# Modulation products moved out of the rounds of five attentions into the two merges of branches

## The reference, cut to what matters

```
# first block: four branches of width 1024
y_fox, y_lru, y_sb, y_mem = ...            # fox and stick-breaking attention, an LRU, memory attention
gates = sigmoid(h @ w_in[:, gates] + b_gate)             # [tokens, 4, 1024]
mixed = sum_n gates[n] * (branches[n] @ w_branch[n])
x = x + mixed @ w_out;  x = x + ffn(x)
# second block: two layers, i = 0, 1
mod  = silu(c)     @ w_ada[i] + b_ada[i]                 # 1024 -> 6 * 1024: shift, scale, gate, twice
modc = silu(c_ctx) @ w_ada[i] + b_ada[i]
h = modulate(rmsnorm(x), sh1, sc1); ...                  # na, da attention and gMLP, width 512 each
x = x + gt1 * ((ga * (ya @ wb[0]) + gb * (yb @ wb[1]) + gc * (yc @ wb[2])) @ w_out)
x = x + gt2 * ec_moe(modulate(rmsnorm(x), sh2, sc2))     # 16 experts
```

## Time and profile before

| | us |
|---|---|
| median of three runs | 3234.0 (3230.39 to 3244.86) |
| the profiled execution's own time | 3241.7 |
| its span in the profile | 3239.9 |
| first merge of branches | 192.0 |
| second merge (layer 0) | 199.0 |
| fox, na_x and da_x attention (layer 0) | 66.9, 64.4, 55.3 |
| mean granted clock of TensorE | 0.925 |

### The profile page before, as it was taken

How to read it: one execution, slowest core, us unless ns; L and a number is a source line. 1 busy time by engine, 2 the same in 40 slices (tenths; PEclk the granted TensorE clock), 3 DMA queues, 4 the chain that set the end, 5 groups by cost and what they waited for, 6 DMA issues and landing times. The chain is left out here.

```text
span 3239.9 us, 36546 instructions
## 1 busy us (share of the span) xinstructions
PE 2658.2 (82%) x14364; PEld 1796.3 (55%) x14364; DVE 1169.5 (36%) x1596; ACT 882.3 (27%) x1314; POOL 39.9 (1%) x36
## 2 busy tenths in 40 slices
PE   6887898998998787889977778887887896787876
PEld 5666687998996464668753222223664894222222
DVE  4446544655753334344432001103444552000001
ACT  3344433544442232322221000002233432000001
POOL 0100000000000000000000000000000001000000
PEclk8888998999998898889978999998897997999999
DMA  4463532453542333112215999996211343999996
GB/s 154 157 257 113 198 130 92 178 185 123 188 159 91 150 136 130 50 69 100 85 46 224 404 405 407 403 414 260 78 52 50 142 165 147 413 410 409 411 410 269
DMA packets 92935, 669.19 MB, mean 207 GB/s; under 512 B 10320, under 2 KB 10496, under 8 KB 12800
## 3 DMA queue, kind: packets, MB, share of 16 engines
q1 hardware_dynamic: 90256, 654.67, 51.6%
q0 software_dynamic: 2272, 11.52, 1.0%
q10 hardware_dynamic: 272, 1.05, 0.1%
HBM read 666.13 MB, written 1.06 MB: 206 GB/s over the span
## 5 line engine op out<-in xcount | busy, mean ns | idle before, releaser
L1860 PE MATMUL ps<-ring,WK 128*64 128x512 f32 x3072 | 731.0, 605 | 171.2 <-DMA ring<-in_stream 147.1
L424 PE MATMUL ps<-A,piece_hi 128*128 128x256 f32 (+1 forms) x1952 | 618.5, 317 | 97.7 <-DVEq L358 33.1
L376 DVE TENSOR_TENSOR ring_lo<-ring,piece_hi 128x1024 fp32r<-128x1024 f32 x378 | 459.3, 1220 | 450.4 <-ACT piece_hi L369 449.3
L425 PE MATMUL ps<-A,piece_hi 128*128 128x256 f32 (+1 forms) x1952 | 612.5, 314 | 0.0
L426 PE MATMUL ps<-A,ring_lo 128*128 128x256 f32 (+1 forms) x1952 | 611.7, 313 | 0.0
L1860 PEld LDWEIGHTS ps<-ring,WK 128*64 128x64 f32 x3072 | 194.5, 137 | 674.2 <-DMA ring<-in_stream 371.9
L424 PEld LDWEIGHTS ps<-A,piece_hi 128*128 128x128 f32 x1952 | 384.7, 197 | 129.3 <-issue 59.2
L369 ACT ACTIVATE piece_hi<-ring 128x1024 fp32r<-128x1024 f32 x378 | 388.2, 1053 | 223.8 <-DVEq L450 131.9
L425 PEld LDWEIGHTS ps<-A,piece_hi 128*128 128x128 f32 x1952 | 385.6, 198 | 17.2
L426 PEld LDWEIGHTS ps<-A,ring_lo 128*128 128x128 f32 x1952 | 384.9, 197 | 18.1
L1980 DVE TENSOR_TENSOR WK<-WK,ps 128x512 f32<-128x512 f32 x32 | 22.0, 688 | 636.7 <-PE ps L1860 636.7
(11 more groups left out here) (252 smaller groups left out, 2447.6 us busy)
## 6 DMA issues: line engine op xcount, KB each, us to landing
ring<-in_stream SPq DMA_DIRECT2D x621, 1024.0 KB, 7.7
WK<-in_na_bias POOLq DMA_DIRECT2D x2, 2048.0 KB, 7.8
WK<-cum_scratch POOLq DMA_DIRECT2D x1, 2048.0 KB, 9.7
const<-in_const SPq DMA_DIRECT2D x1, 1267.0 KB, 11.7
WK<-in_x SPq DMA_DIRECT2D x1, 1024.0 KB, 5.4
WK<-in_mem SPq DMA_DIRECT2D x1, 1024.0 KB, 9.1
WK<-cum_scratch POOLq DMA_DIRECT2D x1, 1024.0 KB, 14.9
WK<-in_lru_w POOLq DMA_DIRECT2D x1, 1024.0 KB, 5.1
```

Of the source, the lines that this page charges most:

```text
L376: nc.vector.tensor_tensor(ring_lo[:, slot, at:at + PIECE], ring[:, slot, at:at + PIECE], f32(piece_hi[:, j, :]), ALU.subtract).then_inc(lo ...
L424: nc.tensor.matmul(out_, l[0], r[0], start=first, stop=False)
L425: nc.tensor.matmul(out_, l[0], r[1], start=False, stop=False)
L1860: last = nc.tensor.matmul(ps[64 * n:64 * n + 64, bank, :], lhs, piece[:, n * 512:n * 512 + 512], start=(k == 0), stop=(k == DC - 1))
```

## The change

The 48 steps of the modulation leave the attentions. A step now follows two split pieces in a merge: 32 steps (four groups, three of layer 0 and the first of layer 1) behind every pair of pieces of the first merge, 16 (two groups) behind the first 16 of 18 pairs of the second. The stream is laid out to match, so that in the first merge every slot of split pieces is followed by a slot of raw ones. `next_piece` and `split_ahead` pass over the raw pieces: still AHEAD = 3 split pieces in front. In these merges the banks go round among six, and the modulation uses banks 6 and 7 in turn. `ada_dve` stands behind each second piece in VectorE's list. The turn and the bias of a group follow one pair later. The first merge is no longer a hardware loop. R, AHEAD and SyncE's code stay as they are.

```diff
+ADA_GROUPS = {0: ((0, 0), (0, 1), (0, 2), (1, 0)), 1: ((1, 1), (1, 2))}
+ADA_NO = {group: n for n, group in enumerate(ADA_GROUPS[0] + ADA_GROUPS[1])}
+def ada_step(merge, slot):
+
+    return (*ADA_GROUPS[merge][slot // DC], slot % DC) if slot < DC * len(ADA_GROUPS[merge]) else None
...
+    def merge(m, slots):
+        nonlocal at
+        for slot in range(slots):
+            at += 2
+            if ada_step(m, slot):
+                RAW[at:at + 2] = ADA
+                at += 2
+                if ada_step(m, slot)[2] == DC - 1:
+                    ADA_LAST[ada_step(m, slot)[:2]] = at - 1
+    merge(0, 32)
+    at += BLOCK_PIECES - 22 * 4 - 64 + 32
+    merge(1, 18)
...
+SPLIT_AT = [p for p in range(PIECES) if RAW[p] == SPLIT]
+SPLIT_NO = np.concatenate([[0], np.cumsum(RAW == SPLIT)])
...
         def split_hi(act, cur):
 
-            j, slot, at = cur.s % 4, cur.s // 2 % R, cur.s % 2 * PIECE
+            no, slot, at = int(SPLIT_NO[cur.s]), cur.s // 2 % R, cur.s % 2 * PIECE
             act.wait_ge(landed[slot], cur.piece_use(cur.s, 1, 16, 2 * R))
-            if cur.s >= 4:
-                act.wait_ge(piece_used[j], cur.piece_use(cur.s))
-            nc.scalar.activation(piece_hi[:, j, :], ring[:, slot, at:at + PIECE], ACT.Copy).then_inc(hi_done[j], 1)
+            if no >= 4:
+                old = SPLIT_AT[no - 4]
+                assert cur.i is None or old == cur.s - 4
+                act.wait_ge(piece_used[old % 4], cur.piece_use(old, 1))
+            nc.scalar.activation(piece_hi[:, no % 4, :], ring[:, slot, at:at + PIECE], ACT.Copy).then_inc(hi_done[no % 4], 1)
             cur.s += 1
...
+        def split_ahead(eng, cur):
+
+            while True:
+                while RAW[cur.s] and cur.s < PIECES:
                     cur.s += 1
-                    continue
+                if cur.s >= PIECES or SPLIT_NO[cur.s] >= SPLIT_NO[cur.p] + AHEAD or cur.s > cur.p + 2 * R - 2:
+                    return
                 if cur.who == "act":
                     split_hi(eng, cur)
-                if cur.who == "dve":
+                elif cur.who == "dve":
                     split_lo(eng, cur)
+                else:
+                    return
+
+        def next_piece(eng, cur, n=1):
+
+            for _ in range(n):
+                assert RAW[cur.p] == SPLIT
+                cur.p += 1
+                while RAW[cur.p] == ADA:
+                    cur.p += 1
+                split_ahead(eng, cur)
...
+        def merge_pe(pe, cur, branches, kc, n, ada=None):
             yh, yl = y_split(kc, n)
-
-            def one_branch(i):
+            slot = 0
+
+            def two_pieces(moving, kc):
+                nonlocal slot
+                fm_banks(pe, cur, moving, n, 2 * DC // kc, kc)
+                if ada is not None:
+                    ada_pe(pe, cur, ada, slot)
+                slot += 1
+
+            for i in range(branches):
                 for h in range(2):
-                    fm_banks(pe, cur, in_a()(n), n, 4)
+                    for _ in range(2):
+                        two_pieces(in_a()(n), DC)
                     if h == 0:
                         pe.wait_ge(y_lo, cur.base("y") + 1 + i)
-                    fm_banks(pe, cur, lambda k: (yh[:, k, :], yl[:, k, :]), n, 4, kc)
-            merge_loop(pe, cur, branches, kc, one_branch)
+                    for _ in range(kc // 4):
+                        two_pieces(lambda k: (yh[:, k, :], yl[:, k, :]), kc)
+            if ada is not None:
+                ada_pe(pe, cur, ada, slot)
             cur.add("y", branches)
...
+            def behind_two():
+                nonlocal slot
+                if ada is not None:
+                    ada_dve(dve, cur, ada, slot)
+                slot += 1
...
-                    dve.wait_ge(bank_free[(cur.g - 1) % NB], cur.bank_use(0 if cur.g % NB == 0 else 1))
+                    for _ in range(2):
+                        skip_fm(dve, cur, 2)
+                        behind_two()
+
+                    dve.wait_ge(bank_free[cur.bank(cur.g - 1)], cur.bank_use(1, cur.g - 1))
                     for j in range(4):
                         def op(bank, j=j):
                             steps(nc.vector.tensor_tensor(GATE[:, j, 0:n], GATE[:, j, 0:n], bank[:, 0:n], ALU.mult))
                             m = MIXT[:, 4 * h + j, 0:n]
                             return nc.vector.tensor_tensor(m, m, GATE[:, j, 0:n], ALU.add)
                         read_bank(dve, cur, True, op, piece=(kc == DC or j % 2 == 1))
+                        if (j + 1) * kc % (2 * DC) == 0:
+                            behind_two()
...
             if k == 0:
-                assert cur.p == ADA_PIECE[layer, g]
                 pe.wait_ge(cs_ready, 1)
-                if n > 0:
-                    pe.wait_ge(ada_added, n)
+                if n >= 2:
+                    pe.wait_ge(ada_added, n - 1)
             for q in range(4):
                 if q % 2 == 0:
                     piece = raw_piece(pe, cur)
-                last = nc.tensor.matmul(ps[32 * q:32 * q + 32, 7, :], CS[:, k, :], piece[:, q % 2 * 512:q % 2 * 512 + 512],
+                last = nc.tensor.matmul(ps[32 * q:32 * q + 32, 6 + n % 2, :], CS[:, k, :], piece[:, q % 2 * 512:q % 2 * 512 + 512],
                                         start=(k == 0), stop=(k == DC - 1))
                 if (k, q) == (DC - 1, 3):
+                    assert cur.p - 1 == ADA_LAST[layer, g]
                     last.then_inc(ada_full, 1)
                 elif q % 2 == 1:
                     raw_used(last, cur)
...
+        def ada_dve(dve, cur, merge, slot):
+            if slot > 0 and ada_step(merge, slot - 1) and ada_step(merge, slot - 1)[2] == DC - 1:
+                layer, g, _ = ada_step(merge, slot - 1)
+                n, lo = ADA_NO[layer, g], layer * MODC + 16 * g
+                dve.wait_ge(ada_turned, n + 1)
+                b = ada_par[:, lo:lo + 16].rearrange("p (q c) -> p c q", q=4).unsqueeze(3).to_broadcast([P, 4, 4, 2])
+                mod = MOD[:, lo:lo + 16, :].rearrange("p (q c) s -> p c q s", q=4)
+                nc.vector.tensor_tensor(mod, ps[:, 6 + n % 2, 0:32].rearrange("p (c q s) -> p c q s", c=4, q=4), b, ALU.add)\
+                    .then_inc(ada_added, 1)
+            if ada_step(merge, slot) and ada_step(merge, slot)[2] == DC - 1:
+                n = ADA_NO[ada_step(merge, slot)[:2]]
+                dve.wait_ge(ada_full, n + 1)
+                dve.sem_inc(piece_used[ADA_LAST[ada_step(merge, slot)[:2]] % 4], 1)
+                if n > 0:
+                    dve.wait_ge(ada_turned, n)
+                nc.vector.tensor_copy(ROWS[:, :], ps[:, 6 + n % 2, :]).then_inc(ada_taken, 1)
...
             att_pe(pe, cur, mem_att)
             barrier(pe, cur)
-            merge_pe(pe, cur, 4, DC, T)
+            cur.set_ring(range(6))
+            merge_pe(pe, cur, 4, DC, T, ada=0)
+            cur.set_ring(range(NB))
...
         for h in range(2):
-            fm(w_in, g0 + n * D + h * 512, g0 + n * D + h * 512 + 512)
-            fm(x["w_branch"][0, n], h * 512, h * 512 + 512)
+            for j, w, at in ((0, w_in, g0 + n * D), (1, w_in, g0 + n * D), (2, x["w_branch"][0, n], 0), (3, x["w_branch"][0, n], 0)):
+                at += h * 512 + j % 2 * 256
+                fm(w, at, at + 256)
+                ada(0, 8 * n + 4 * h + j)
```

More of the change, by code:

```diff
@@ L136, in __init__ @@
         self.g = 0
+        self.places = []
+        self.ring = list(range(NB))
+        self.turn = 0
+        self.uses = [0] * NB
         self.i = None
@@ L154, in split_use, with place, set_ring, used @@
     def split_use(self, piece, k=0):
-        v = (piece - int(RAW_BEFORE[piece])) // 4 + k
+        v = int(SPLIT_NO[piece]) // 4 + k
         return v if self.i is None else v + self.i * (self.pieces_per // 4)
-    def bank(self):
-        return self.g % NB
-    def bank_use(self, k=0):
-        v = self.g // NB + k
+    def place(self, g):
+        while len(self.places) <= g:
+            b = self.ring[self.turn % len(self.ring)]
+            self.places.append((b, self.uses[b]))
+            self.uses[b] += 1
+            self.turn += 1
+        return self.places[g]
+    def set_ring(self, banks):
+        while len(self.places) < self.g:
+            self.place(len(self.places))
+        assert len(self.places) == self.g, (self.who, len(self.places), self.g)
+        self.ring, self.turn = list(banks), 0
+    def used(self, bank):
+        self.place(self.g - 1)
+        return sum(b == bank for b, _ in self.places[:self.g])
+    def bank(self, g=None):
+        return self.place(self.g if g is None else g)[0]
+    def bank_use(self, k=0, g=None):
+        v = self.place(self.g if g is None else g)[1] + k
         return v if self.i is None else v + self.i * self.banks_per
+    def taken_before(self):
+        return self.place(self.g)[1] > 0
 def one(i):
@@ L485, in tm_tile @@
         def tm_tile(pe, cur, t0, tt):
-            banks = [(cur.g + m) % NB for m in range(tt)]
```

(27 more changed lines are left out.)

244 lines of the change are left out of this document (93 added, 151 removed).

## The result

Changed kernel: 3253.2 us (median of 8 runs, 3237.3 to 3254.9). Kernel before, on the same chip: 3234.1 (8 runs, 3228.8 to 3247.8). The ratio is 1.0048, 95% interval 1.0027 to 1.0070: 19 us dearer where I forecast 64. That lies in my range of 3245 to 3350, low in it, but outside the 3280 to 3320 that I gave for the forecast itself: it is in the range only by the room left for a rival. It lies at the edge of what I called no change, with a chance of 0.14: the ratio is under 0.5%, the difference of the medians is 0.6%, and 3253.2 is above the 3250 at which I ended it.

What follows compares the result with a forecast made beforehand. Merges were taken as bound by TensorE, attentions as chains of three engines. Attentions -58, first merge +103, second +19 made +64 us on 3234: 3298, rounded to 3300 us (own range 3280 to 3320; overall range 3245 to 3350).

Steps and rivals of the forecast that it cites:

- What the attentions give back: Attention stages without their 48 steps and six turns: 62.6 us saved, less 5 for splits moved to earlier stages, 58 us.
- twin: Layer 1's same stage without steps, used to price na_x (64.4 against 53.1 us) and da_x (55.3 against 47.0).
- The second merge: 16 steps and two turns on a saturated TensorE cost 19 us; late releases there cost nothing.
- The term of the step, 1.05: TensorE's time for one step in a merge, 1.05 us, used as 16 x 1.05 in the second merge.
- The first merge: Paced by late refills of the four-slot ring, not by the steps: 295 us against 192.0, +103 us.
- So each release hangs on the last: First merge: in-order engines wait for a landing before releasing the next slot, so releases follow after 7.3 to 13.3 us.
- The loop written out costs nothing: First merge without its hardware loop: priced at nothing, as the second merge is written out and TensorE busy 99%.
- 13.3 us at a new branch: First merge, between branches: release interval including two table loads and the 1.9 us copy, in place of 8.8.
- Only the gate chain binds: Rival: every first-merge release takes 7.3 us, the merge 252 us, the kernel 3255; chance 0.11.
- 9.25: First merge: us until the next release when a branch pair comes next, with VectorE releasing after two splits, multiply and add.
- The ring keeps up: Rival: refills ready in 7.85 us, merges pay 57 us for 58 saved in the attentions, kernel 3233; chance 0.12.
- The clock: First merge: full clock forecast; the rival had half the pairs at half clock, 46 us more, 3345; chance 0.11.

## Why the prediction was off
- **What the attentions give back** came out right in the sum, 60 us for 58, in part by luck. Single stages missed by up to 4.4 us both ways. Of the 5 us for splits that move to the stages before, the profile has 2.3 (0.8 in the projection before sb, 1.1 before na_x, 0.4 before da_x), and the stages behind fox, sb's projection and da_x (LRU, memory attention, da_ctx) are 2.4, 2.6 and 2.0 us shorter, which I had not seen; each is within what two profiles differ by. Na_x kept 57.6 us where its twin had taken 53.1: without steps it is granted 0.67 of the clock, as its twin in the same profile, 56.3 us at 0.73. A twin's time holds for its clock.
- **The second merge** was right: +21.3 for 19. The term of the step, 1.05, is 1.18: 16 x 1.18 and two turns make 21. I had the bound 0.96 to 1.4 for it.
- **The first merge** is where it failed, 249.5 us for 295, at the step "So each release hangs on the last" and its bullets. The order is as I said: ScalarE waits for a landing behind every pair, and the merge follows that chain (252 us even when TensorE has 18 us less to do, 229 when the wait is moved one piece back). But I let each count wait for all work in front of it in its engine's list, and it is made 1.2 to 1.3 us earlier, while the engine has a read and a split yet to do. 32 releases by 1.3 us are 42, an estimate: it takes all 32 for links of the chain, and by the trace 12 of them waited for nothing but the full bank. Drains in front of the counts gave 299.5, with their own cost in it.
- **"The loop written out costs nothing"** missed a gain: 5.0 us. My 13.3 us at a new branch held two table loads that only the loop has, 2.6 us in each branch, 10 in all; with the 42 my 295 become 243. What is missing to 249.5 I can't assign from one number; the waits for the row copies, 10 us, are of that size.
- **The account of the first merge**, from what the runs measured: 192.0 - 5.0 for the loop, + 32 x 1.18 = 37.8 for the steps, + some 5 for four turns (the changed kernel's L1546 is busy 5.2) make 229.8; with splits two ahead it was 229.4. The remaining 20 us of the 249.5 are the engines' lists held by the waits for landings.
- **The rivals.** "Only the gate chain binds" gave 3255 and 252 us for the merge, near what came. But not for its reason: the refill at a branch pair that the chain holds follows after 7.7 us (538.94 to 546.67), more than the gate chain's 7.3 and less than 9.25, because its count is early. "The ring keeps up" (3233) is what the changed kernel becomes with one number changed, 3233.9. The clock did not fall: 0.99.

## What to carry to other kernels
When loads, splits and reads stand in one in-order list, ask for the split of a freshly released slot as late as its use allows: one piece less of looking ahead was worth 20 us here, and no edit of who makes the releases was. Work moved from an attention into a saturated merge is not free even if its loads are: it costs TensorE more than its matmuls (1.18 us for what has 0.87 of matmuls), and what it gives back in the attention is loads and hand-overs and not matmuls, so price both sides by stage. A loop in hardware can make an engine reload its tables in each pass; write out a short one where that engine releases a ring.

## What the runs showed of the hardware
- A count on a semaphore by an engine's queue (`sem_inc`) was seen 1.3 us (ScalarE) and 1.2 us (VectorE) before the engine began the read behind it, with a split still in work. A drain in front of it takes that away.
- A step among full-size matmuls cost TensorE 0.31 us in the first merge beside its own matmuls, and 0.35 to 0.44 us were saved in the second for each change to 32-column tiles and back that was spared; that the change of tiles is the cause fits both and is not shown alone.
- TensorE's granted clock in na_x was 0.81 with the steps and 0.67 without: work taken out of a stage of many pauses (TensorE busy 8 us less in na_x, 48.2 to 40.2) can be partly paid back in clock. It is no rule: with their steps gone da_x fell from 0.86 to 0.78 and sb from 0.89 to 0.79, but fox rose from 0.81 to 0.86 and na_ctx went from 0.85 to 0.86.
